# Token-wise input projection in six groups of 432 columns, with the 16 step columns inside the sixth

## The chip, the cores and the metric

The kernel runs on one core of a Trainium2 chip. The time is device microseconds of one launch, median of several runs; less is better. The engines are named as in the profile: PE is TensorE (PEld its weight loads), DVE is VectorE, ACT is ScalarE, POOL is GpSimd, and SP only issues DMA transfers and waits.

## The reference, cut to what matters

One layer of a diffusion backbone over 128 context and 1024 latent tokens. Everything is float32.

```python
h = rmsnorm(x, ln1_w) * (1 + sc1) + sh1                 # 1152 tokens x 1024
proj = h @ w_in                                         # 1024 x 3600
z, xbc, dt_raw, rq, rk, rv, rg = split(proj, [512, 1536, 1552, 2064, 2576, 3088])
xbc = silu(depthwise_conv_centred(xbc, conv_w, conv_b)) # 5 taps over tokens
dt_f = softplus(dt_raw[..., :8] + dt_bias_f)            # the 16 step columns
...                                                     # scans, w_out, PEER
```

The change touches the product `h @ w_in` alone, and there the columns outside `xbc`: z, the 16 step columns `dt_raw`, and the four retention parts, 2576 columns in all.

## The kernel before, in words

`project_in` is one block of the program (all engines meet at its start and at its end). It holds the transposed activations `hT`, eight slices of 128 features by 1152 tokens (T = 9 x 128, NT = 9). Every float32 operand is split in two, a rounded `_hi` and a remainder `_lo` (called `_rest` in the profile), and every product is three matmuls (hi x hi, hi x lo, lo x hi) for each of the KD = 8 slices: 24 matmuls to a result tile. ACT makes the `_hi` of a weight tile (`split_x`, `split_t`), DVE its remainder (`rest_x`, `rest_t`), and only then can PE use it.

The work comes in three parts, which PE does in this order.

1. *Channel blocks.* The 1024 `xbc` columns in NB = 8 blocks of 128. PE fills three PSUM banks of 384 tokens (72 matmuls), banks 0 to 2 for even blocks and 3 to 5 for odd ones. ACT copies them out (`copy_in`), DVE makes the convolution (`conv`, five operations), ACT the silu (`silu`), SP stores the block to `xbc_d`.
2. *Step columns.* The 16 columns `dt_raw` by themselves: for each of nine token tiles 24 matmuls of 16 moving columns, L423 (216 in all), into bank 6; weights `wd`, result `dts`.
3. *Token-wise groups.* The other 2560 columns in five groups of 512 (`group`, L436): for each of nine token tiles 24 matmuls of 512 columns into one of NQ = 3 banks; ACT copies the tile into one of three buffers `st`, SP stores it to `tok_d`. Tile 3 of a group can start once tile 0 is copied, and ACT can copy into a buffer once the store of three tiles before has landed (`st_stored`).

Each engine keeps the order of its own code. SP's order matters here: it stores all eight convolved blocks, waiting for each silu, then issues the first two loads of the modulation weights (`load_mod`, tile `wmr`), and then for each tile of the groups a further modulation load and the tile's store:

```python
for grp in range(5):
    for t in range(NT):
        if 2 <= grp * NT + t < 4 * KD:
            load_mod(grp * NT + t)          # waits until DVE is done with load n-2
        sp.wait_ge(tile_copied, grp * NT + t + 1)
        sp.dma_start(g.tok_d[...], st[t % NQ][:])
```

DVE works the 32 modulation rows off (L568) between the `rest_t` of the weight groups: after rows 7, 15 and 23 it waits for `split_t` of group 2, 3 and 4. POOL loads the weights, group j+2 when PE has finished group j. ACT does `split_t(j + 2)` after it has copied the last tile of group j.

Of the kernel before, what the change touches and what calls it, by code (L numbers as in the profile page):

```python
# [39 lines left out]
TC = PROJ - XBC  # L40
# [242 lines left out]
def twin(nc, ctx, name, shape):  # L283

    off = nc.sbuf_base
    assert off % 32 == 0
    whole = ctx.enter_context(nc.sbuf_tensor(name, shape, F32))
    return whole, nc.alloc_sbuf_tensor_at(name + "_rest", shape, F32R, offset=off)


def project_in(nc, g):
# [7 lines left out]
    NQ = 3  # L299
    with ExitStack() as ctx:  # L300
# [10 lines left out]
        wt, wt_lo = zip(*(twin(nc, ctx, f"wt{i}", [P, KD, 512]) for i in range(2)))  # L311
        wt_hi = [sb(f"wt_hi{i}", [P, KD, 512], F32R) for i in range(2)]
        (wd, wd_lo), wd_hi, dts = twin(nc, ctx, "wdt", [P, KD, 16]), sb("wdt_hi", [P, KD, 16], F32R), sb("dts", [P, NT, 16])
        st = [sb(f"st{i}", [P, 512]) for i in range(NQ)]
        padded, chain_sem, chain_sem_v = sem("padded"), sem("chain"), sem("chainv")
        small, wd_loaded, wx_loaded, wt_loaded = g.pi_small, g.pi_wd, g.pi_wx, g.pi_wt
# [3 lines left out]
        dt_done, dt_copied, dt_stored = sem("dt"), sem("dtcopied"), sem("dtstored")  # L320
        tile_done, tile_copied, group_done = sem("tile"), sem("tilecopied"), sem("group")
        st_stored = [sem(f"st{i}") for i in range(NQ)]
        wv = g.w_in.rearrange("(k p) n -> p k n", p=P)
# [6 lines left out]
        wx_hi_ready, wx_lo_ready, wd_hi_ready, wd_lo_ready, wt_hi_ready, wt_lo_ready = (  # L330
            sem(n) for n in ("wxhi", "wxlo", "wdhi", "wdlo", "wthi", "wtlo"))
# [4 lines left out]
        def groups(eng, body):  # L336

            body(0, 0)
            with eng.Fori(0, 2) as i:
                body(i * 2 + 1, 1)  # L340
                body(i * 2 + 2, 0)

        @block.gpsimd
        def _(pool):
            for s in range(2):
                for a, b in ((0, PAD), (PAD + P, 3 * PAD + P), (WID - PAD, WID)):
                    pool.memset(pre[s][:, a:b], 0.0).then_inc(padded, 1)
            pool.dma_start(cw[:], g.conv_w_cols).then_inc(small, 16)
            pool.dma_start(cb[:], g.conv_b_cols).then_inc(small, 16)
            for s in range(2):  # L350
                pool.dma_start(wx[s][:], wv[:, :, 512 + s * P:512 + (s + 1) * P]).then_inc(wx_loaded[s], 16)
            pool.dma_start(wd[:], wv[:, :, 512 + XBC:REST0]).then_inc(wd_loaded, 16)
            pool.dma_start(wt[0][:], wv[:, :, 0:512]).then_inc(wt_loaded[0], 16)
            pool.dma_start(wt[1][:], wv[:, :, REST0:REST0 + 512]).then_inc(wt_loaded[1], 16)
            with pool.Fori(0, NB // 2 - 1) as i:
                for s in range(2):
                    pool.wait_ge(block_done, i * 2 + s + 1)
                    pool.dma_start(wx[s][:], wv[:, :, bass.ds(i * (2 * P) + (512 + (2 + s) * P), P)]).then_inc(wx_loaded[s], 16)
            for j in range(3):
                pool.wait_ge(group_done, j + 1)  # L360
                c = REST0 + (j + 1) * 512
                pool.dma_start(wt[j % 2][:], wv[:, :, c:c + 512]).then_inc(wt_loaded[j % 2], 16)

        @block.sync
        def _(sp):
            for seq in range(2):
                sp.dma_start(cb2[:, seq], bcast_rows(g.c_rows[seq])).then_inc(mod_small, 16)
            sp.dma_start(bcol[:], g.b_mod_cols).then_inc(mod_small, 16)
            sp.dma_start(lnc[:], g.ln_cols[:, 1]).then_inc(mod_small, 16)
            for s in range(2):  # L370
                sp.sem_inc(cv_stored[s], 16)
            for s in range(NQ):
                sp.sem_inc(st_stored[s], 16)
            with sp.Fori(0, NB // 2) as i:
                for s in range(2):
                    sp.wait_ge(silu_done, i * 2 + s + 1)
                    sp.dma_start(g.xbc_d[bass.ds(i * (2 * P) + s * P, P), :], cv[s][:]).then_inc(cv_stored[s], 16)
            sp.wait_ge(dt_copied, 1)
            sp.dma_start(g.tok_d[:, 5 * 512:].rearrange("(t p) c -> p t c", p=P), dts[:]).then_inc(dt_stored, 16)

            def load_mod(n):
                if n >= 2:
                    sp.wait_ge(mod_done, 2 * (n - 1))
                sp.dma_start(wm[n % 2][:], g.w_modT[n]).then_inc(wm_loaded[n % 2], 16)
            load_mod(0)
            load_mod(1)
            for grp in range(5):
                for t in range(NT):
                    if 2 <= grp * NT + t < 4 * KD:
                        load_mod(grp * NT + t)  # L390
                    sp.wait_ge(tile_copied, grp * NT + t + 1)
                    sp.dma_start(g.tok_d[t * P:(t + 1) * P, bass.ds(grp * 512, 512)], st[t % NQ][:]).then_inc(st_stored[t % NQ], 16)
# [7 lines left out]
            sp.wait_ge(dt_stored, 16)  # L400
            for s in range(NQ):
                sp.wait_ge(st_stored[s], 16 * (5 * NT // NQ + 1))

        @block.tensor
        def _(pe):
# [12 lines left out]
            pe.wait_ge(wd_lo_ready, 1)  # L418
            for t in range(NT):
                rows = slice(t * P, (t + 1) * P)  # L420
                for k in range(KD):
                    for m, (h, w) in enumerate(((h_hi, wd_hi), (h_hi, wd_lo), (g.hT_lo, wd_hi))):
                        mm = pe.matmul(g.ps[6][:, 16 * t:16 * t + 16], h[:, k, rows], w[:, k, :],  # L423
                                       start=(k == 0 and m == 0), stop=(k == KD - 1 and m == 2))
            mm.then_inc(dt_done, 1)
            pe.wait_ge(banks_free, NB + 2)

            def group(grp, s):
                pe.wait_ge(wt_lo_ready, grp + 1)
# [19 lines left out]
        def _(act):  # L449
# [42 lines left out]
            act.wait_ge(wd_loaded, 16)  # L492
            act.activation(wd_hi[:], wd[:], ACT.Copy).then_inc(wd_hi_ready, 1)
# [10 lines left out]
            def group(grp, s):  # L504
                for t in range(NT):
                    act.wait_ge(tile_done, grp * NT + t + 1)
                    act.wait_ge(st_stored[t % NQ], grp * (16 * NT // NQ) + (t // NQ) * 16 + 16)
                    act.activation(st[t % NQ][:], g.ps[t % NQ][:], ACT.Copy).then_inc(tile_copied, 1)
            for grp in range(5):
                group(grp, grp % 2)  # L510
                if grp < 3:
                    split_t(grp + 2)

        @block.vector
        def _(dve):
# [38 lines left out]
            dve.wait_ge(wd_hi_ready, 1)  # L554
            dve.tensor_tensor(wd_lo[:], wd[:], f(wd_hi[:]), ALU.subtract).then_inc(wd_lo_ready, 1)
# [6 lines left out]
            for j in range(2, 6):  # L562
# [7 lines left out]
                if j < 5:  # L570
                    rest_t(j)
# [14 lines left out]
def decay_terms(nc, g):  # L586
# [4 lines left out]
    with ExitStack() as ctx:  # L591
# [17 lines left out]
        def _(sp):  # L609
            for dst, src in ((x[:, 0:NT, :], g.tok_d[:, 5 * 512:].rearrange("(t p) c -> p t c", p=P)),  # L610
# [1373 lines left out]
def program(nc, g, ctx):  # L1984
# [3 lines left out]
    g.pi_small, g.pi_wd, g.pi_wx, g.pi_wt = sem("pi_small"), sem("pi_wd"), [sem(f"pi_wx{i}") for i in range(2)], [sem(f"pi_wt{i}") for i in range(2)]  # L1988
# [130 lines left out]
```

## Time and profile before

| | us |
|---|---|
| median of 3 runs | 3805.85 (3803.96 to 3814.33) |
| the profiled execution: its own time | 3806.96 |
| the profiled execution: span of the core | 3805.2 |
| `project_in` within the span | about 78 to 491 |
| PE busy | 3415.7 (90%) |
| DVE busy | 2887.7 (76%) |
| ACT busy | 1418.4 (37%) |

Times in the profile are microseconds from the start of the span. The granted clock (PEclk) is the share of 2.4 GHz that PE was given: 1.00 is 2.4 GHz and 0.50 is 1.2 GHz. An idle entry such as "8.53 <-PE ps L423" says that the engine sat idle for 8.53 us until that work released it.

### The profile page before, as it was taken

The numbers are of one execution on the slowest core, as the hardware profiler recorded it, in microseconds if no ns is written. First come the engines' busy times: TensorE is split into PE (matmuls) and PEld (weight loads), VectorE is DVE, ScalarE is ACT, GpSimd is POOL, SyncE is SP. The second block draws the span as 40 slices with busy tenths as digits, with TensorE's granted clock in tenths as the row PEclk, the third lists the DMA queues.
The fourth block names the chain that finished last, engine by engine and source line by source line (L and its number), as shares of the span: only waits on it lengthen the run. The fifth ranks groups of instructions, "written<-read, shape, count | busy, mean of one in ns | idle before, by whom it ended". The sixth has DMA issues, their size and how long they took to land. (4 is left out here: it accounts for less than half of the span.)

```text
span 3805.2 us, 52216 instructions
## 1 busy us (share of the span) xinstructions
PE 3415.7 (90%) x17854; PEld 2993.1 (79%) x17854; DVE 2887.7 (76%) x4884; ACT 1418.4 (37%) x2552; POOL 1770.8 (47%) x1003
## 2 busy tenths in 40 slices
PE   5999969697999999999889899997997998989998
PEld 2998859444999999899888888996776776767776
DVE  4544247595578899998999999657886888878886
ACT  2321135243222222224777777523332333333332
POOL 0000012110211778786888888765554654555510
PEclk8979989798999999999999999998998999999999
DMA  5225334542112778776989888879999999989976
GB/s 197 74 84 180 114 105 144 167 143 80 34 34 66 233 247 257 242 262 230 341 331 348 329 342 334 329 271 356 361 384 358 354 357 353 363 327 375 371 270 210
DMA packets 416593, 947.30 MB, mean 249 GB/s; under 512 B 38035, under 2 KB 230211, under 8 KB 413267
## 3 DMA queue, kind: packets, MB, share of 16 engines
q1 hardware_dynamic: 293252, 457.63, 35.9%
q0 software_dynamic: 114480, 417.47, 29.9%
q10 hardware_dynamic: 8736, 70.78, 4.8%
q8 instruction: 48, 0.79, 0.1%
q14 instruction: 77, 0.62, 0.1%
HBM read 807.65 MB, written 138.11 MB: 249 GB/s over the span
## 5 line engine op out<-in xcount | busy, mean ns | idle before, releaser
L1872 POOL DMA_INDIRECT hT<-peer_v,hT x336 | 595.6, 1773 | 487.3 <-DVE hrow L1884 408.1
L1725 PE MATMUL ps<-h_hi,u_hi 128*128 128x384 f32 x2048 | 699.0, 341 | 31.0 <-POOL u_lo L1611 23.2
L1725 PE MATMUL ps<-h_lo,u_hi 128*128 128x384 f32 x2048 | 689.0, 336 | 0.0
L1725 PE MATMUL ps<-h_hi,u_lo 128*128 128x384 f32 x2048 | 689.0, 336 | 0.0
L1962 PE MATMUL ps<-v_hi,a_hi 128*128 128x512 f32 x1512 | 487.2, 404 | 125.8 <-DVE ga_rest L1896 114.9
L1962 PE MATMUL ps<-vw_rest,a_hi 128*128 128x512 f32 x1512 | 476.4, 397 | 0.0
L1962 PE MATMUL ps<-v_hi,ga_rest 128*128 128x512 f32 x1512 | 474.6, 396 | 0.0
L1962 PEld LDWEIGHTS ps<-v_hi,a_hi 128*128 128x128 f32 x1512 | 283.3, 193 | 219.6 <-DVE vw_rest L1894 147.0
L1842 ACT ACTIVATE v_hi<-vw 128x1024 fp32r<-128x1024 f32 x256 | 270.6, 1057 | 410.9 <-DMA vw<-peer_v 399.1
L1607 POOL DMA_INDIRECT hT<-u_rows,hT x224 | 376.0, 1679 | 95.8 <-issue 51.2
L1884 DVE SCALAR_TENSOR_TENSOR hrow<-hT,dots,hrow 128x1024 f32<-128x1024 f32 x336 | 420.4, 1279 | 0.0
L1611 POOL TENSOR_TENSOR u_lo<-uw,u_hi 128x1024 fp32r<-128x1024 f32 x126 | 341.7, 2712 | 160.8 <-ACT u_hi L1518 159.6
L1725 PEld LDWEIGHTS ps<-h_hi,u_hi 128*128 128x128 f32 x2048 | 388.2, 190 | 34.8 <-issue 32.0
L1725 PEld LDWEIGHTS ps<-h_lo,u_hi 128*128 128x128 f32 x2048 | 388.4, 190 | 0.0
L1725 PEld LDWEIGHTS ps<-h_hi,u_lo 128*128 128x128 f32 x2048 | 387.7, 189 | 0.0
L1962 PEld LDWEIGHTS ps<-vw_rest,a_hi 128*128 128x128 f32 x1512 | 290.9, 192 | 63.3
L1632 DVE CUSTOM_DVE_ANT_0 hT<-hT,hrow 128x1024 f32<-128x1024 f32 x224 | 314.0, 1446 | 33.2 <-DMA hT<-u_rows,hT 32.1
L1962 PEld LDWEIGHTS ps<-v_hi,ga_rest 128*128 128x128 f32 x1512 | 289.6, 192 | 62.9
L1523 ACT ACTIVATE so<-ps 128x384 f32<-128x384 f32 x256 | 123.8, 484 | 544.0 <-PE ps L1725 417.8
L1892 DVE TENSOR_TENSOR ga<-ga,gt 128x384 f32<-128x384 f32 x256 | 142.0, 555 | 241.0 <-DMA ga<-s_d 239.1
L1894 DVE TENSOR_TENSOR vw_rest<-vw,v_hi 128x1024 fp32r<-128x1024 f32 x256 | 312.3, 1220 | 9.7 <-ACT v_hi L1842 8.6
L1691 DVE TENSOR_TENSOR hT<-iota,sel 128x1024 f32<-128x1024 f32 x192 | 302.7, 1616 | 6.4 <-ACT sel L1546 6.4
(336 smaller groups left out, 6040.2 us busy)
## 6 DMA issues: line engine op xcount, KB each, us to landing
vw<-peer_v SPq DMA_DIRECT2D x256, 512.0 KB, 8.5
uw<-u_T SPq DMA_DIRECT2D x128, 512.0 KB, 4.3
s_d<-so SPq DMA_DIRECT2D x256, 192.0 KB, 5.0
gates_d<-big ACTq DMA_DIRECT2D x24, 2048.0 KB, 10.0
gt<-gates_d SPq DMA_DIRECT2D x64, 768.0 KB, 8.8
ga<-s_d SPq DMA_DIRECT2D x256, 192.0 KB, 8.8
wmr<-w_modT SPq DMA_DIRECT2D x32, 512.0 KB, 4.0
tok_d<-st SPq DMA_DIRECT2D x45, 256.0 KB, 2.2
```

The source lines that it names most:

```text
L1523: act.activation(so[b][:], g.ps[4 + 2 * s + b][:, 0:HALF], ACT.Gelu_apprx_tanh).then_inc(act_done, 1)
L1607: pool.indirect_dma_start(rows[slot], None, table, bass.IndirectOffsetOnAxis(ap=g.pick[q][:, i:i + 1], axis=0)).then_inc(row_loaded[slot], 16)
L1611: pool.tensor_tensor(u_lo[e % 2][:], uw[e % 2][:], f(u_hi[e % 2][:]), ALU.subtract).then_inc(u_lo_ready, 1)
L1632: z = dve.tensor_tensor_reduce(rows[slot], rows[slot], g.hrow[:, n // NSEL], 1.0, 0.0, ALU.mult, ALU.add, g.dots[:, n // NSEL, n % NSEL:n ...
L1691: z = dve.tensor_tensor(hot, numbers, sel3[:, i, r * G:(r + 1) * G].unsqueeze(2).broadcast_to([P, G, P]), ALU.is_equal)
L1725: mm = pe.matmul(g.ps[4 + 2 * s + b][:, 0:HALF], u[s][:, k, :], h[:, k, b * HALF:(b + 1) * HALF], start=(k == 0 and i == 0), stop=(k == KD ...
L1842: act.activation(v_hi[s][:], vw[s][:], ACT.Copy).then_inc(v_hi_ready, 1)
L1872: pool.indirect_dma_start(rows[n % NU], None, g.v_rows, bass.IndirectOffsetOnAxis(ap=g.pick[m % GT][:, m // GT:m // GT + 1], axis=0)).then ...
L1884: dve.scalar_tensor_tensor(g.hrow[:, q], rows[n % NU], g.dots[:, q, i:i + 1], g.hrow[:, q], ALU.mult, ALU.add).then_inc(added, 1)
L1892: dve.tensor_tensor(by, by, gt[n // RING % 2][:, 0:(c1 - c0) // CT, s * CT:(s + 1) * CT], ALU.mult).then_inc(a_ready, 1)
L1894: dve.tensor_tensor(v_lo[s][:], vw[s][:], f(v_hi[s][:]), ALU.subtract).then_inc(v_lo_ready, 1)
L1962: mm = pe.matmul(g.ps[bank(p, t) + q][:], aa[s][:, rows_], v[s][:, q * 512:(q + 1) * 512], start=(begin and i == 0), stop=(end and i == 2) ...
```

## The change

The step columns lose their own pass. The 2576 columns outside `xbc`, with the step columns last and 16 columns of zeros behind them, make six groups of 432 (`TW`). The zeros and the new order of columns are laid out ahead of the launch, in two inputs `w_xbc` and `w_tok` in place of `w_in`. So there are 54 tiles of 24 matmuls of 432 columns in place of 45 tiles of 512 and the 216 matmuls of 16. Ahead of group 0 PE waits until channel block 6 (of 0 to 7) is copied out of banks 0 to 2 (`banks_free` NB + 1), and no longer until block 7 is. ACT copies the first three tiles of group 0 ahead of the last silu.

```diff
@@ -37,7 +37,8 @@
-TC = PROJ - XBC
+TW = 432
+TC = 6 * TW
...
         def groups(eng, body):
 
             body(0, 0)
-            with eng.Fori(0, 2) as i:
+            body(1, 1)
+            with eng.Fori(1, NG // 2) as i:
+                body(i * 2, 0)
                 body(i * 2 + 1, 1)
-                body(i * 2 + 2, 0)
...
             for s in range(2):
-                pool.dma_start(wx[s][:], wv[:, :, 512 + s * P:512 + (s + 1) * P]).then_inc(wx_loaded[s], 16)
-            pool.dma_start(wd[:], wv[:, :, 512 + XBC:REST0]).then_inc(wd_loaded, 16)
-            pool.dma_start(wt[0][:], wv[:, :, 0:512]).then_inc(wt_loaded[0], 16)
-            pool.dma_start(wt[1][:], wv[:, :, REST0:REST0 + 512]).then_inc(wt_loaded[1], 16)
+                pool.dma_start(wx[s][:], wv[:, :, s * P:(s + 1) * P]).then_inc(wx_loaded[s], 16)
+            for j in range(2):
+                pool.dma_start(wt[j][:], tv[:, :, j * TW:(j + 1) * TW]).then_inc(wt_loaded[j], 16)
...
-            for j in range(3):
-                pool.wait_ge(group_done, j + 1)
-                c = REST0 + (j + 1) * 512
-                pool.dma_start(wt[j % 2][:], wv[:, :, c:c + 512]).then_inc(wt_loaded[j % 2], 16)
+            for j in range(2, NG):
+                pool.wait_ge(group_done, j - 1)
+                pool.dma_start(wt[j % 2][:], tv[:, :, j * TW:(j + 1) * TW]).then_inc(wt_loaded[j % 2], 16)
...
-            sp.wait_ge(dt_copied, 1)
-            sp.dma_start(g.tok_d[:, 5 * 512:].rearrange("(t p) c -> p t c", p=P), dts[:]).then_inc(dt_stored, 16)
...
-            pe.wait_ge(wd_lo_ready, 1)
-            for t in range(NT):
-                rows = slice(t * P, (t + 1) * P)
-                for k in range(KD):
-                    for m, (h, w) in enumerate(((h_hi, wd_hi), (h_hi, wd_lo), (g.hT_lo, wd_hi))):
-                        mm = pe.matmul(g.ps[6][:, 16 * t:16 * t + 16], h[:, k, rows], w[:, k, :],
-                                       start=(k == 0 and m == 0), stop=(k == KD - 1 and m == 2))
-            mm.then_inc(dt_done, 1)
-            pe.wait_ge(banks_free, NB + 2)
+            pe.wait_ge(banks_free, NB + 1)
...
             copy_in(NB - 2, 0, NB // 2 - 1)
-            act.wait_ge(wd_loaded, 16)
-            act.activation(wd_hi[:], wd[:], ACT.Copy).then_inc(wd_hi_ready, 1)
             split_t(0)
             silu(NB - 2, 0, NB // 2 - 1)
             copy_in(NB - 1, 1, NB // 2 - 1)
             split_t(1)
+
+            def group(grp, tiles):
+                for t in tiles:
+                    act.wait_ge(tile_done, grp * NT + t + 1)
+                    act.wait_ge(st_stored[t % NQ], grp * (16 * NT // NQ) + (t // NQ) * 16 + 16)
+                    act.activation(st[t % NQ][:], g.ps[t % NQ][:, 0:TW], ACT.Copy).then_inc(tile_copied, 1)
+            group(0, range(NQ))
             silu(NB - 1, 1, NB // 2 - 1)
             act.wait_ge(mod_small, 64)
             act.activation(cb2[:], cb2[:], ACT.Silu).then_inc(mod_silu, 1)
-            act.wait_ge(dt_done, 1)
-            act.activation(dts[:], g.ps[6][:, 0:16 * NT].rearrange("p (t c) -> p t c", t=NT), ACT.Copy).then_inc(dt_copied, 1)
...
-            for grp in range(5):
-                group(grp, grp % 2)
-                if grp < 3:
+            for grp in range(NG):
+                group(grp, range(NQ if grp == 0 else 0, NT))
+                if grp + 2 < NG:
                     split_t(grp + 2)
...
-            dve.wait_ge(wd_hi_ready, 1)
-            dve.tensor_tensor(wd_lo[:], wd[:], f(wd_hi[:]), ALU.subtract).then_inc(wd_lo_ready, 1)
...
-            for dst, src in ((x[:, 0:NT, :], g.tok_d[:, 5 * 512:].rearrange("(t p) c -> p t c", p=P)),
+            for dst, src in ((x[:, 0:NT, :], g.tok_d[:, 5 * 512:5 * 512 + 16].rearrange("(t p) c -> p t c", p=P)),
...
-        "w_in": A["w_in"][0],
+        "w_xbc": f(A["w_in"][0][:, 512:512 + XBC]),
+        "w_tok": f(np.concatenate([A["w_in"][0][:, 0:512], A["w_in"][0][:, REST0:], A["w_in"][0][:, 512 + XBC:REST0],
+                                   np.zeros((D, TC - (PROJ - XBC)), np.float32)], 1)),
```

PE, at the end of the channel blocks (ps5 is the last bank of block 7, ps6 was the bank of the step columns). Before:

```order
L415 MATMUL ps5<-hT_rest_49,wx_hi1 128x384
L415 MATMUL ps5<-pi_h_hi,wx1_rest_498 128x384
L406 REGISTER_ALU
L406 COMPARE_AND_BRANCH
L423 MATMUL ps6<-wdt_hi,pi_h_hi 128x16 [waits pi_wdlo]
L423 MATMUL ps6<-wdt_rest_501,pi_h_hi 128x16
```

And PE at the same place now:

```order
L410 MATMUL ps5<-hT_rest_49,wx_hi1 128x384
L410 MATMUL ps5<-pi_h_hi,wx1_rest_498 128x384
L401 REGISTER_ALU
L401 COMPARE_AND_BRANCH
L423 MATMUL ps0<-wt_hi0,pi_h_hi 128x432 [waits pi_wtlo,pi_banksfree]
L423 MATMUL ps0<-wt0_rest_499,pi_h_hi 128x432
```

The first tile of group 0 now stands right behind the last channel block, where the 216 matmuls of the step columns stood.

ACT, from the split of group 0's weights on (wt0 and wt1 are the weights of groups 0 and 1, cv0 and cv1 the convolved blocks 6 and 7; between them block 7 is copied out). Before:

```order
L493 ACTIVATE wdt_hi<-wdt 128x128 [waits pi_pre,pi_wd]
L458 ACTIVATE wt_hi0<-wt0 128x4096 [waits pi_wt0]
L481 ACTIVATE cv0<-acc0,cb 128x128 [waits pi_cvst0,pi_conv]
...
L458 ACTIVATE wt_hi1<-wt1 128x4096 [waits pi_pre,pi_wt1]
L481 ACTIVATE cv1<-acc1,cb 128x128 [waits pi_cvst1,pi_conv]
L482 ACTIVATE cv1<-acc1,cb 128x1024
L500 ACTIVATE cboth<-cboth 128x2048 [waits pi_chain,pi_msmall]
L502 ACTIVATE dts<-ps6 128x144 [waits pi_dt]
```

And ACT at the same place now:

```order
L445 ACTIVATE wt_hi0<-wt0 128x3456 [waits pi_pre,pi_wt0]
L468 ACTIVATE cv0<-acc0,cb 128x128 [waits pi_cvst0,pi_conv]
...
L445 ACTIVATE wt_hi1<-wt1 128x3456 [waits pi_pre,pi_wt1]
L488 ACTIVATE st0<-ps0 128x432 [waits pi_st0,pi_tile]
L488 ACTIVATE st1<-ps1 128x432 [waits pi_st1,pi_tile]
L488 ACTIVATE st2<-ps2 128x432 [waits pi_st2,pi_tile]
L468 ACTIVATE cv1<-acc1,cb 128x128 [waits pi_cvst1,pi_conv]
L469 ACTIVATE cv1<-acc1,cb 128x1024
```

Three tile copies moved ahead of the last silu; the split of `wdt` and the copy of `dts` are gone.

SP, behind the loop that stores the convolved blocks. Now it reads (before, one more row, the store of `dts`, stood ahead of the first `wmr` load):

```order
L375 DMA xbc_d<-cv1 128x1152
L372 REGISTER_ALU
L372 COMPARE_AND_BRANCH
L380 DMA wmr0<-w_modT 128x1024
L380 DMA wmr1<-w_modT 128x1024
L388 DMA tok_d<-st0 128x432 [waits pi_tilecopied]
L388 DMA tok_d<-st1 128x432 [waits pi_tilecopied]
```

SP's order did not move with ACT's: the stores of the first tiles still stand behind the store of the last convolved block.

## Rows read from the trace of the kernel before

**Rows 1.** The page: its first line.

```profile
span 3805.2 us, 52216 instructions
```

**Rows 2.** Instructions by line: PE, times in ns min/median/max, then first and last start.

```profile
L423 PE MATMUL ps<-wdt_hi,pi_h_hi x72: 170/361/362, 194.3 to 236.1; 128*128 128x16 f32 x72
L436 PE MATMUL ps<-wt_hi,pi_h_hi x360: 388/388/774, 236.8 to 489.2; 128*128 128x512 f32 x180
```

**Rows 3.** Busy time by stretch: length, busy (count) per engine, PEclk, DMA share, GB/s.

```profile
88.30:92.30 4.00, 3.97 (x12) 3.97 (x13) 2.60 (x1) 4.00 (x3) 0.00 (x0) 0.50 1.02 419
92.30:198.10 105.80, 102.49 (x600) 101.53 (x599) 53.53 (x41) 36.79 (x55) 5.34 (x6) 1.00 0.24 83
198.10:236.90 38.80, 38.80 (x184) 38.80 (x185) 19.53 (x12) 9.72 (x10) 0.00 (x0) 0.50 0.08 31
236.90:242.50 5.60, 5.60 (x15) 4.34 (x15) 0.57 (x1) 0.29 (x1) 0.00 (x0) 0.50 0.71 199
```

**Rows 4.** Timeline of ACT: start, length, operation, count, [idle before it, who ended it].

```profile
192.07 0.31 ACT L493 ACTIVATE wdt_hi<-wdt 128x128 fp32r<-128x128 f32 x1
192.29 3.61 ACT L458 ACTIVATE wt_hi<-wt 128x4096 fp32r<-128x4096 f32 x1
...
210.14 3.62 ACT L458 ACTIVATE wt_hi<-wt 128x4096 fp32r<-128x4096 f32 x1
...
225.18 1.13 ACT L482 ACTIVATE cv<-acc,cb 128x1024 f32<-128x1024 f32 x1
```

**Rows 5.** Timeline of ACT in the groups: the copies of tiles.

```profile
245.24 0.60 ACT L508 ACTIVATE st<-ps 128x512 f32<-128x512 f32 x1 [8.01 <-PE ps L436]
250.73 0.60 ACT L508 ACTIVATE st<-ps 128x512 f32<-128x512 f32 x1 [4.89 <-PE ps L436]
...
490.12 0.60 ACT L508 ACTIVATE st<-ps 128x512 f32<-128x512 f32 x1 [4.89 <-PE ps L436]
```

**Rows 6.** Timeline of POOL: loads issued when channel blocks 1 and 2 are done.

```profile
116.08 0.88 POOL L358 DMA_DIRECT2D wx<-w_in  x1 [11.55 <-PE ps L415]
128.58 0.88 POOL L358 DMA_DIRECT2D wx<-w_in  x1 [11.61 <-PE ps L415]
```

**Rows 7.** Timeline of DVE: the remainders of groups 0 and 1, the last convolution.

```profile
195.93 4.43 DVE L525 TENSOR_TENSOR wt_rest<-wt,wt_hi 128x4096 fp32r<-128x4096 f32 x1 [3.22 <-ACT wt_hi L458]
...
213.79 4.43 DVE L525 TENSOR_TENSOR wt_rest<-wt,wt_hi 128x4096 fp32r<-128x4096 f32 x1 [6.87 <-ACT wt_hi L458]
...
218.98 5.80 DVE L544 SCALAR_TENSOR_TENSOR acc<-pre,cw,acc 128x1156 f32<-128x1156 f32 x4
```

**Rows 8.** Timeline of SP: last block's store, first modulation loads; then load 26.

```profile
226.53 0.33 SPq L377 DMA_DIRECT2D xbc_d<-cv  x1
...
237.69 1.07 SPq L384 DMA_DIRECT2D wmr<-w_modT  x2
...
408.36 0.33 SPq L384 DMA_DIRECT2D wmr<-w_modT  x1
```

**Rows 9.** Page, DMA issues: transfer, size, median us to landing.

```profile
tok_d<-st SPq DMA_DIRECT2D x45, 256.0 KB, 2.2
```

**Rows 10.** Timeline of ACT at the end of group 2 (tile 26) and behind it.

```profile
389.54 0.60 ACT L508 ACTIVATE st<-ps 128x512 f32<-128x512 f32 x1 [4.90 <-PE ps L436]
397.96 3.63 ACT L458 ACTIVATE wt_hi<-wt 128x4096 fp32r<-128x4096 f32 x1 [7.83 <-DMA wt<-w_in]
...
413.31 0.60 ACT L508 ACTIVATE st<-ps 128x512 f32<-128x512 f32 x1 [10.75 <-DMA tok_d<-st]
416.51 0.60 ACT L508 ACTIVATE st<-ps 128x512 f32<-128x512 f32 x1 [2.60 <-DMA tok_d<-st]
```

**Rows 11.** Tile wt, issue to landing of the five weight loads.

```profile
DMA to landing us min/median/max: 8.0/10.3/14.4
```

**Rows 12.** Tile wx, 70 to 200 us: waits that its load ended (us, times).

```profile
  DMA wx<-w_in: 8.6, 2
```

**Rows 13.** Waits in 190 to 495 us: total, times, longest.

```profile
ACT st L508 <- DMA tok_d<-st: 22.9, 4, 10.8
```

More of the change, by code:

```diff
@@ L299, in project_in @@
     NQ = 3
+    NG = TC // TW
     with ExitStack() as ctx:
@@ L310, in project_in @@
         cw, cb = sb("cw", [P, NB, TAPS]), sb("cb", [P, NB])
[L311 to L314, printed above, removed]
+        wt, wt_lo = zip(*(twin(nc, ctx, f"wt{i}", [P, KD, TW]) for i in range(2)))
+        wt_hi = [sb(f"wt_hi{i}", [P, KD, TW], F32R) for i in range(2)]
+        st = [sb(f"st{i}", [P, TW]) for i in range(NQ)]
         padded, chain_sem, chain_sem_v = sem("padded"), sem("chain"), sem("chainv")
-        small, wd_loaded, wx_loaded, wt_loaded = g.pi_small, g.pi_wd, g.pi_wx, g.pi_wt
+        small, wx_loaded, wt_loaded = g.pi_small, g.pi_wx, g.pi_wt
         block_done, banks_free, pre_ready, pre_free = sem("block"), sem("banksfree"), sem("pre"), sem("prefree")
@@ L319, in project_in @@
         cv_stored = [sem("cvst0"), sem("cvst1")]
-        dt_done, dt_copied, dt_stored = sem("dt"), sem("dtcopied"), sem("dtstored")
         tile_done, tile_copied, group_done = sem("tile"), sem("tilecopied"), sem("group")
         st_stored = [sem(f"st{i}") for i in range(NQ)]
-        wv = g.w_in.rearrange("(k p) n -> p k n", p=P)
+        wv, tv = (w.rearrange("(k p) n -> p k n", p=P) for w in (g.w_xbc, g.w_tok))
         wm, cb2 = [sb(f"wmr{i}", [P, D]) for i in range(2)], sb("cboth", [P, 2, D])
@@ L329, in project_in @@
         h_hi_ready, h_lo_ready = sem("hhi"), sem("hlo")
-        wx_hi_ready, wx_lo_ready, wd_hi_ready, wd_lo_ready, wt_hi_ready, wt_lo_ready = (
-            sem(n) for n in ("wxhi", "wxlo", "wdhi", "wdlo", "wthi", "wtlo"))
+        wx_hi_ready, wx_lo_ready, wt_hi_ready, wt_lo_ready = (sem(n) for n in ("wxhi", "wxlo", "wthi", "wtlo"))
         f = lambda ap: ap.bitcast(F32)
@@ L391, in _ @@
                     sp.wait_ge(tile_copied, grp * NT + t + 1)
-                    sp.dma_start(g.tok_d[t * P:(t + 1) * P, bass.ds(grp * 512, 512)], st[t % NQ][:]).then_inc(st_stored[t % NQ], 16)
+                    sp.dma_start(g.tok_d[t * P:(t + 1) * P, grp * TW:(grp + 1) * TW], st[t % NQ][:]).then_inc(st_stored[t % NQ], 16)
             sp.wait_ge(mod_rows, 1)
@@ L431, in group @@
                     rows = slice(t * P, (t + 1) * P)
-                    if not (isinstance(grp, int) and t < NQ):
+                    if not (isinstance(grp, int) and grp * NT + t < NQ):
                         pe.wait_ge(tile_copied, grp * NT + (t - NQ + 1))
@@ L435, in group @@
                         for m, (h, w) in enumerate(((h_hi, wt_hi), (h_hi, wt_lo), (g.hT_lo, wt_hi))):
-                            mm = pe.matmul(g.ps[t % NQ][:], h[:, k, rows], w[s][:, k, :],
+                            mm = pe.matmul(g.ps[t % NQ][:, 0:TW], h[:, k, rows], w[s][:, k, :],
                                            start=(k == 0 and m == 0), stop=(k == KD - 1 and m == 2))
@@ L500, in _ @@
             act.activation(cb2[:], cb2[:], ACT.Silu).then_inc(mod_silu, 1)
-            act.wait_ge(dt_done, 1)
-            act.activation(dts[:], g.ps[6][:, 0:16 * NT].rearrange("p (t c) -> p t c", t=NT), ACT.Copy).then_inc(dt_copied, 1)
[L504 to L509, printed above, removed]
-                group(grp, grp % 2)
-                if grp < 3:
+            for grp in range(NG):
+                group(grp, range(NQ if grp == 0 else 0, NT))
+                if grp + 2 < NG:
                     split_t(grp + 2)
@@ L1987, in program @@
     sem = lambda n: new_sem(nc, ctx, n, lasting)
-    g.pi_small, g.pi_wd, g.pi_wx, g.pi_wt = sem("pi_small"), sem("pi_wd"), [sem(f"pi_wx{i}") for i in range(2)], [sem(f"pi_wt{i}") for i in range(2)]
+    g.pi_small, g.pi_wx, g.pi_wt = sem("pi_small"), [sem(f"pi_wx{i}") for i in range(2)], [sem(f"pi_wt{i}") for i in range(2)]
     g.hg_rows, g.ou_rows = [sem(f"hg_row{i}") for i in range(16)], [sem(f"ou_row{i}") for i in range(NU)]
```

8 lines of the change are left out of this document (3 added, 5 removed).

## Prediction

> **What bounds the kernel now.** I read the page's first line, then the lines of PE, then the stretches of `project_in`, and last the timelines of ACT, DVE and SP around its weak places. The profiled execution took 3806.96 us for a span of 3805.2 [rows 1], 1.1 us over the median of 3805.85. `project_in` ends with all engines meeting, so what PE gains in it should be gained at the end, unless a later stage gives it back.
>
> The step columns hold PE from 194.3 to 236.8 [rows 2]: 42.5 us for 216 matmuls of 16 columns. The reader should see in [rows 3] what they do to the clock: 1.00 up to 198.1, 0.50 until 236.9, and still 0.50 for 5.6 us after the wide matmuls have begun. The groups follow until the last tile is copied at 490.12 [rows 5]. Tiles are 5.49 us apart (245.24, 250.73), 228.9 ns for each of 24 matmuls. From the first copy to the last, 244.88 us hold 44 tiles (241.7) and four joints between groups, 3.2 together. So PE bounds the groups and almost nothing stalls it.
>
> **The change, part by part.**
>
> *Removed: the step columns.* Their 42.5 us go, with the slow start of group 0 behind them (its first copy comes 8.4 us after 236.8, not 5.5: 2.9 us). The split of `wdt` (0.31 [rows 4]), its load, and the copy and store of `dts` lay beside other work; I count them as 0 except the 0.22 us that ACT was later for it (192.29 for 192.07).
>
> *Wider in number, narrower each: the tiles.* No row has 432 columns. Those of 384 are in the channel blocks: 12.50 us from block 1 to block 2 [rows 6] for 72 matmuls, 173.6 ns each. A line from there to 228.9 at 512 gives 194.3 ns at 432, a tile of 4.66 us. The bounds are in proportion to columns from either end, 4.63 and 4.69. So 54 tiles take 251.6 us where 45 took 247.2: +4.4 us (2.8 to 6.1).
>
> The page "TensorE: Matmul & The Clock Gate" of the Trainium skill (Back-to-back issue gap) has columns over 2.4 GHz and 2.5 ns for every matmul. By it 54 tiles would take 236.5 us and 45 tiles 233.1, a difference of 3.4 in place of 4.4. Its 215.8 ns for 512 columns is below the 228.9 of this trace, so the trace agrees that a fixed part is small, not with the size.
>
> *The new start of group 0.* PE is done with block 7 at 194.3 and then waits for the remainder of group 0's weights. ACT starts their split at 192.07, in 3.61 x 432/512 = 3.05 us; DVE's remainder [rows 7] takes 4.43 x 432/512 = 3.74; so PE starts at 192.07 + 3.05 + 3.74 + 0.1 = 198.95. Block 6 was copied out before 192.07, so the bank wait is free. PE idles 4.65 us. Tiles 0 to 5 end at 198.95 + 6 x 4.66 = 226.9.
>
> *ACT's first tiles.* DVE was free of group 0's remainder at 200.36 and will be at 198.9: what follows from it comes 1.46 us earlier. The split of group 1's weights starts at 208.7 (was 210.14 [rows 4]) and ends at 211.75. Tile 2 ends at 212.9, so all three copies are made by 213.5, tiles 3 to 5 need no wait, and the last silu is not late for it: DVE's second remainder ends at 215.5, and the last convolution, which ended 6.56 us behind that (224.78 against 218.22 [rows 7]), at 222.1. The silu ended 1.53 us behind it (226.31 [rows 4]), now at 223.7.
>
> *The new wait, on SP's queue.* ACT can copy tile 3 only when the store of tile 0 has left buffer 0, and SP issues that store behind the last convolved block and two modulation loads. By its spacing in [rows 8] (block 0.2 after the silu, two loads in 1.07): block 223.9, loads 224.3 and 224.9, tile 0 at 225.4. When it lands no row shows. Not before 225.4 + 2.2 [rows 9] = 227.6, if it passes the loads. From above: load 26 issued at 408.36 [rows 8] and the store behind it ended ACT's wait at 413.31, the next pair at 416.51 [rows 10]: 4.95 us for 768 KB and 3.2 for each further 768. Block, loads and store are 1816 KB from 223.9, so 4.95 + 1048/240 = 9.3, landing at 233.2. I take 231.0, nearer the upper end, since it is queued behind the loads. ACT's copy is done at 231.65; PE needed it at 226.9 for tile 6. **Stall 4.75 us** (1.4 to 6.9). Behind this copy on ACT are those of tiles 4 and 5; their stores follow at once or some 5 us later, and PE needs them 4.66 and 9.3 us later, in time.
>
> *The clock after the two gaps.* Gaps in the channel blocks left 1.00 [rows 3]; longer idle time ahead of 88.3 and the step columns left 0.50 for 4.0 and 5.6 us of work, which costs half, 2.0 to 2.8. A fall after the first gap is hidden, since tile 6 waits for the store anyway; one after the second is not. I take half its price, 1.2.
>
> The same page (Why this matters for your kernels) tells authors to leave no idle gaps between bursts of matmuls, or the clock falls back. Its rule speaks against this change, which makes two gaps where there was none. By it both gaps cost, and the sum is 1.2 us worse than mine, 3778; which gap is long enough no run here shows yet.
>
> *Later groups.* The tightest place is tile 32, the sixth of group 3. It needs tile 29's copy, that the store of tile 26, that load 26, that DVE's row 24, that the remainder of group 4's weights, whose load starts as group 2 ends. Before: group end 389.54, split 397.96, load 26 at 408.36, copy at 413.31, done 24.4 us after the end; PE came at 0.8 + 5 x 5.49 = 28.3, a joint and five tiles. Now split and remainder are 1.25 shorter and the load about 1.2, so 22.0, and PE comes after 0.8 + 5 x 4.66 = 24.1. Slack 2.1 us, for a load 8.0 long [rows 11]. At 10.9 it would be overrun by 0.3 us, at 14.4 by 3.3.
>
> *At nothing.* The channel blocks' weights now come from rows 4096 bytes apart in place of 14400, and group weights in pieces of 1728 bytes in place of 2048. Only two `wx` loads ended a wait (8.6 us [rows 12]); the others hide behind DVE and ACT. A load 1 us longer or shorter costs or gives 2 us. The modulation rows end long before PE does.
>
> **Sum.** Tile 6 starts at 231.7; 48 tiles take 223.7 and five joints 4.0 (the four had 3.2): 459.4, and 460.6 with the clock's 1.2. Against 490.1 that is 29.5 us less: 3806.96 - 29.5 = 3777.5. I put 3777.
>
> **The rivals.**
>
> 1. *SP's queue is not late* (13%). The store passes the loads and lands near 227.6; tile 6 starts at 228.3, and the clock stays high. Then PE ends at 456.0, 34.1 less: **3772.9**. For it: a tile store alone takes 2.2 us. Against it: with a load ahead, ACT waited up to 10.8 us for one [rows 13].
>
> 2. *The waits spread* (20%). Store at 233.2 (+2.2), the whole fall of the clock (+1.6), and loads of weights as long as the long ones in [rows 11], with 3.3 at tile 32 and about 1 elsewhere: +8.1, **3785.6**. For it: ACT already waited 22.9 us in four such places [rows 13]; its cover shrinks with the tile. Against it: PE still has 2 us there, and the traffic per group is smaller.
>
> 3. *A matmul of 432 columns costs what one of 512 does* (3%), the case on the other side. Each tile then takes 5.49: tile 6 starts at 231.9 and 48 tiles take 263.5, PE ends at 499.4 and with the clock's 1.2 at 500.6: +10.5 us, **3817**. It decides from (490.1 - 460.6)/1152 = 26 ns more per matmul, 220 ns. Against it: 384 columns take 173.6, on the line through 512 and nearly nothing.
>
> 4. *Loads from the new rows are much slower* (2%). Only two are on the path now; the others must first use up their cover. To eat 29.5 us all eight must land at least 29.5/8 = 3.7 us later, and more by what the six now have in hand. About **3800** to 3810. Against it: the same bytes in the same number of pieces.
>
> My forecast has 62%, with a range of its own from 3772 to 3783.
>
> **How the numbers follow.** Rivals 1 and 2 lie on either side and are both faster; 3 and 4 are left out of the range. The stages behind 491 us run the same instructions, but three runs of before spread from 3804 to 3814, so a few us are added: 3768 to 3790. What can be told from no change is 0.3%, 11.4 us, so faster means below 3794: my forecast and rivals 1 and 2, 95%, less 1 for a later stage that gives it back. Same 3%, slower 3% (rival 3).
>
> **What the changed profile would show.** The first wide matmul near 199 after a gap of 4.65; 4.66 us between copies; tile 3's copy near 231 with a wait that ends on a transfer of `tok_d`; a second gap of PE of 1 to 7 us ahead of tile 6; the last copy near 460; no stall of PE in group 3. Wrong if copies are over 4.75 apart, if the second gap is absent or above 7, or if the span behind the last copy is not about 3315 us, as it was (3805.2 - 490.1).

## The result and the profile after

| | median us | lowest to highest | runs | profiled execution | span |
|---|---|---|---|---|---|
| before | 3814.06 | 3803.96 to 3818.05 | 10 | 3806.96 | 3805.2 |
| changed | 3788.77 | 3778.29 to 3798.79 | 10 | 3781.83 | 3780.2 |

The ratio is 0.9939 (95%: 0.9922 to 0.9956): faster, by more than the 0.3% that can be told. The medians differ by 25.3 us and the two profiled executions by 25.1; the forecast was 28.9. The median lies outside the range that the forecast gave itself, 3772 to 3783, and inside the wider 3768 to 3790. Two things differ from the forecast, and they are kept apart below: the saving, a few us smaller, and the level of both kernels. The seven runs added for the kernel before lifted its median by 8.2 us, from 3805.85 to 3814.06.

First the stage of the change. The windows of the changed kernel from the end of the last channel block on (length, busy time and count for PE, PEld, DVE, ACT, POOL, then PEclk, DMA share, GB/s); they answer to [rows 3]:

```profile
194.30:198.97 4.67, 0.05 (x1) 0.03 (x1) 3.90 (x2) 0.73 (x1) 0.00 (x0) 0.91 0.00 0
198.97:204.70 5.73, 5.73 (x16) 5.28 (x17) 5.59 (x5) 0.00 (x0) 0.00 (x0) 0.50 0.00 0
204.70:229.95 25.25, 25.25 (x130) 24.04 (x128) 11.24 (x8) 10.59 (x13) 0.00 (x0) 0.99 0.25 87
229.95:232.04 2.09, 0.17 (x2) 0.00 (x1) 2.09 (x5) 0.56 (x2) 0.00 (x0) 1.00 0.61 231
232.04:235.60 3.56, 3.56 (x10) 3.26 (x11) 2.21 (x4) 0.51 (x1) 0.00 (x0) 0.54 0.73 172
```

The 38.8 us at half clock and the slow start behind them are gone. In their place stand two gaps of PE, and behind each a stretch at 0.50 and 0.54, the level of 1.2 GHz for all or nearly all of it. The first wide matmul and the second gap, from the timeline of PE in the same trace:

```profile
198.97 0.70 PE L423 MATMUL ps<-wt_hi,pi_h_hi 128*128 128x432 f32 x1 [4.62 <-DVE wt_rest L509]
...
232.04 0.53 PE L423 MATMUL ps<-wt_hi,pi_h_hi 128*128 128x432 f32 x1 [1.93 <-ACT st L488]
```

The wait behind that gap, from the timeline of ACT:

```profile
211.62 0.93 ACT L488 ACTIVATE st<-ps 128x432 f32<-128x432 f32 x2
216.11 0.53 ACT L488 ACTIVATE st<-ps 128x432 f32<-128x432 f32 x1 [3.56 <-PE ps L423]
...
222.47 1.14 ACT L469 ACTIVATE cv<-acc,cb 128x1024 f32<-128x1024 f32 x1
...
231.46 1.09 ACT L488 ACTIVATE st<-ps 128x432 f32<-128x432 f32 x2 [5.75 <-DMA tok_d<-st]
```

and the timeline of SP, whose queue the store of tile 0 stood in; it answers to [rows 8]:

```profile
223.82 0.33 SPq L375 DMA_DIRECT2D xbc_d<-cv  x1
224.37 1.25 SPq L380 DMA_DIRECT2D wmr<-w_modT  x2
225.66 0.93 SPq L388 DMA_DIRECT2D tok_d<-st  x2
```

ACT had copied tile 0 before 213, but SP issued its store at 225.66, behind the last convolved block and two loads, and ACT stood still until 231.46 (forecast 231.0). The copy was early, but its store was not. The rest of the stage is steady, as [rows 5] was; ACT's copies:

```profile
277.15 0.53 ACT L488 ACTIVATE st<-ps 128x432 f32<-128x432 f32 x1 [3.43 <-PE ps L423]
281.83 0.53 ACT L488 ACTIVATE st<-ps 128x432 f32<-128x432 f32 x1 [4.15 <-PE ps L423]
...
356.71 0.53 ACT L488 ACTIVATE st<-ps 128x432 f32<-128x432 f32 x1 [9.89 <-DMA tok_d<-st]
...
462.76 0.53 ACT L488 ACTIVATE st<-ps 128x432 f32<-128x432 f32 x1 [4.15 <-PE ps L423]
```

Tiles are 4.68 us apart, and the last copy is at 462.76 where it was at 490.12, 27.4 us earlier in the span. Counted from the start of the projection, which came 0.4 us earlier (78.0 for 78.4), the stage is 26.9 us shorter. Behind the last copy the span goes on for 3317.4 us, where it went on for 3315.1: 2.3 us less saved at the end.

### The profile page after: what moved, and what is told of

The parts are those of the page before. It is cut to its first block and busy times, and to the rows that moved or that the text cites. A ratio compares the mean times of both kernels' runs of the same rounds, so it can differ in the third digit from the quotient of the medians.

```text
span 3780.2 us, 52243 instructions
## 1 busy us (share of the span) xinstructions
PE 3380.7 (89%) x17854; PEld 2991.9 (79%) x17854; DVE 2888.3 (76%) x4884; ACT 1418.9 (38%) x2560; POOL 1746.4 (46%) x1003
## 5 line engine op out<-in xcount | busy, mean ns | idle before, releaser
L1853 POOL DMA_INDIRECT hT<-peer_v,hT x336 | 575.6, 1713 | 509.3 <-DVE hrow L1865 434.6
L1943 PEld LDWEIGHTS ps<-v_hi,a_hi 128*128 128x128 f32 x1512 | 284.4, 193 | 220.9 <-DVE vw_rest L1875 131.1
```

What stands on the lines that cost most here:

```text
L1853: pool.indirect_dma_start(rows[n % NU], None, g.v_rows, bass.IndirectOffsetOnAxis(ap=g.pick[m % GT][:, m // GT:m // GT + 1], axis=0)).then ...
L1943: mm = pe.matmul(g.ps[bank(p, t) + q][:], aa[s][:, rows_], v[s][:, q * 512:(q + 1) * 512], start=(begin and i == 0), stop=(end and i == 2) ...
```

## The experiments

Each profile is cut at one place, the last tile copy. "Stage" is the time from the start of the input projection to that copy, and "behind" the rest of the span. "Outputs" is the last stage of the program, part of "behind", and "DVE waits" what DVE stands still in it for the loads of `ga`. Medians compare only within a row: groups of kernels ran on different chips, each beside the kernel before on the same chip. Ahead of the stage lie 78.0 to 82.5 us in the twelve profiles.

| kernel | median, runs | before it | ratio (95%) | stage | behind | outputs | DVE waits |
|---|---|---|---|---|---|---|---|
| before | 3814.06, 10 | | | 411.7 | 3315.1 | 1227.8 | 219.2 |
| before_again | 3815.6, 1 | | | 412.2 | 3321.4 | 1233.3 | 225.0 |
| before_third | 3818.2, 1 | | | 412.0 | 3325.2 | 1236.8 | 227.4 |
| changed | 3788.77, 10 | 3814.06 | 0.9939 (0.9922 to 0.9956) | 384.8 | 3317.4 | 1230.5 | 221.7 |
| after_again | 3802.48, 12 | 3822.11 | 0.9939 (0.9914 to 0.9965) | 386.1 | 3308.5 | 1217.2 | 207.8 |
| early | 3794.37, 6 | 3822.11 | 0.9916 (0.9885 to 0.9947) | 372.9 | 3329.3 | 1239.8 | 231.2 |
| sp_first | 3791.12, 6 | 3822.11 | 0.9912 (0.9879 to 0.9944) | 381.9 | 3331.5 | 1247.1 | 238.3 |
| act_undo | 3803.38, 10 | 3822.11 | 0.9951 (0.9925 to 0.9977) | 392.4 | 3327.0 | 1238.4 | 229.8 |
| one_step | 3796.9, 10 | 3823.0 | 0.9946 (0.9920 to 0.9972) | 385.7 | 3327.8 | 1239.5 | 231.1 |
| one_step_order | 3780.93, 4 | 3823.0 | 0.9895 (0.9855 to 0.9935) | 376.0 | 3318.8 | 1230.1 | 220.9 |
| fill | 3783.6, 1 | | | 386.8 | 3314.2 | 1225.9 | 217.5 |
| both | 3781.54, 6 | 3820.02 | 0.9901 (0.9865 to 0.9937) | 374.0 | 3327.0 | 1237.5 | 229.1 |

The intervals of the ratios all overlap: the medians show that each of these kernels is faster than the one before, and not which of them is fastest. What follows is read from the stage, one profile to a kernel; the stage repeats within 1.3 us in two profiles of the changed kernel and within 0.5 in three of the kernel before.

### early: the splits ahead of the channel blocks

The edit to the changed kernel, on ACT and the same on DVE:

```diff
             act.wait_ge(small, 32)
+            split_t(0)
+            split_t(1)
...
-            split_t(0)
             silu(NB - 2, 0, NB // 2 - 1)
             copy_in(NB - 1, 1, NB // 2 - 1)
-            split_t(1)
...
             dve.wait_ge(small, 32)
+            rest_t(0)
+            rest_t(1)
...
-            rest_t(0)
             conv(NB - 2, 0)
-            rest_t(1)
             conv(NB - 1, 1)
```

> The changed kernel with the splits of the weights of groups 0 and 1 (ACT and DVE) moved ahead of the first channel block, where both engines idle. Theory A, the ledger of the prediction as measured (gap of 4.6 us, then the store of tile 0 late on SP, then two falls of the clock): PE goes straight from block 7 at 194 into group 0, every later step of ACT, DVE and SP comes 7 to 10 us earlier (last silu near 210, tile 0 stored near 217), no wait at tile 6; 54 tiles of 4.68 and joints of 4.2: last copy at 451, 12 us before the changed kernel's 462.8. Rival B, that only the removal of the step columns matters and the gaps are made good by slack later on: last copy at 461 to 463. Time: A 0.3% under the changed kernel, 0.9% under the kernel before; B as the changed kernel.

Its windows over the same work, with the same columns:

```profile
194.00:200.00 6.00, 6.00 (x35) 5.96 (x35) 3.57 (x3) 1.95 (x5) 0.00 (x0) 1.00 0.24 98
...
222.00:262.00 40.00, 39.70 (x204) 37.87 (x203) 24.96 (x38) 8.20 (x11) 0.88 (x1) 1.00 0.65 198
```

PE is busy all the way and the clock stays at 1.00. The stage takes 372.9 us, 11.9 less than the changed kernel's. The store wait on ACT is still there (its copy of tile 3 is at 222.67, after 5.79 us idle for `tok_d`), but ACT's and DVE's work ahead of it is shorter, so it ends before PE needs the bank. The two gaps and what the clock lost behind them were 12 us that PE could have worked: 4.62 and 1.93 us of idle time, 2.9 and 1.6 us lost at the lower clock, 11.1 of the 11.9.

### after_again: the changed kernel once more

No edit.

> The changed kernel once more, beside the kernel before on the same chip, for the level that the prediction missed. Theory A: inside the groups nothing varies but the clock; last copy at 462 to 464 again, and the stages behind differ from run to run by several us with the clock that PE is granted in them, so the ratio is again 0.992 to 0.995, while both absolute medians may lie anywhere within 10 us of the first ones. Rival B: the later stages systematically give back some 2 to 4 us of the gain; then the span behind the last copy is again at least 3317 against 3315 of before.

The stage repeats within 1.3 us (386.1 and 384.8), the ratio to four digits. Behind the last copy it takes 3308.5 us, less than the kernel before (3315.1): nothing there gives the saving back. On this chip the medians of both kernels are higher than in the first comparison, by 8.1 (before) and 13.7 us (changed).

### sp_first: the first stores ahead of the last block and the loads

```diff
-            with sp.Fori(0, NB // 2) as i:
+            with sp.Fori(0, NB // 2 - 1) as i:
...
+            sp.wait_ge(silu_done, NB - 1)
+            sp.dma_start(g.xbc_d[(NB - 2) * P:(NB - 1) * P, :], cv[0][:]).then_inc(cv_stored[0], 16)
+            for t in range(NQ):
+                sp.wait_ge(tile_copied, t + 1)
+                sp.dma_start(g.tok_d[t * P:(t + 1) * P, 0:TW], st[t][:]).then_inc(st_stored[t], 16)
+            sp.wait_ge(silu_done, NB)
+            sp.dma_start(g.xbc_d[(NB - 1) * P:NB * P, :], cv[1][:]).then_inc(cv_stored[1], 16)
...
+                    if grp * NT + t < NQ:
+                        continue
```

> The changed kernel with SP storing tiles 0 to 2 of group 0 ahead of the last convolved block and the modulation loads. Theory A (tile 6 waits for the store of tile 0 behind the block and two loads): tile 3 is copied as soon as ACT is through with the last silu and cboth, near 225.8, and PE goes from tile 5 (230.2 after the first fall of the clock) into tile 6 without a gap and without the second fall: the last copy 1.9 + 1.7 = 3.6 us earlier, 459.1. Rival B (tile 6 waits for ACT, not for the store): ACT's copy of tile 3 stays near 231.5 and the last copy at 462.8. Rival C: the modulation rows now start later and push DVE's remainders, so that a later group stalls: last copy at 461 or more though the first wait is gone.

The timeline of ACT in this kernel, with tiles 3 and 4, then tile 6:

```profile
226.07 0.93 ACT L497 ACTIVATE st<-ps 128x432 f32<-128x432 f32 x2
...
238.89 0.54 ACT L497 ACTIVATE st<-ps 128x432 f32<-128x432 f32 x1 [7.89 <-DMA tok_d<-st]
```

Tile 3 is copied at 226.07 behind no transfer, the second gap and the second fall of the clock are gone (from 226 to 262 us PE works 35.42 of 36.00 us at a granted clock of 1.00), and the stage is 2.9 us shorter than the changed kernel's (4.2 against its repeat). That is the price of SP's order. The wait has moved three tiles on, to a store behind the modulation loads, where PE has more in hand.

### act_undo: the last silu first again

```diff
-            group(0, range(NQ))
             silu(NB - 1, 1, NB // 2 - 1)
...
             act.activation(cb2[:], cb2[:], ACT.Silu).then_inc(mod_silu, 1)
+            group(0, range(NQ))
```

> The changed kernel with ACT's first three tile copies put back behind the last silu and the silu of cboth, the order of before. Theory A: tile 3 cannot start before ACT has done cboth at 225.7, and copies tile 0 at 226.3; PE idles from 216.1 for 10 us, the clock falls again (1.7 to 2.8 us), tiles 3 to 5 end near 242 to 243, tile 3's store wait is over by then; last copy 8 to 11 us later, 471 to 474. The silu comes no earlier, since it waits for DVE. Rival B (ACT is free enough; DVE's silu order does not matter): within 2 us of 462.8.

PE now waits at tile 3, for the copy of tile 0:

```profile
229.02 0.73 PE L423 MATMUL ps<-wt_hi,pi_h_hi 128*128 128x432 f32 x1 [10.08 <-ACT st L488]
```

The stage is 392.4 us, 6.3 to 7.6 more than the changed kernel's two runs. The mechanism is as expected, its price a little below the 8 us that were expected at least. The order on ACT is thus worth about 7 of the 27 us by which the changed stage is shorter.

### one_step and one_step_order: the old kernel with a ninth of the step pass

Both start from the kernel before. one_step:

```diff
-            for t in range(NT):
+            for t in range(1):
                 rows = slice(t * P, (t + 1) * P)
...
-            act.activation(dts[:], g.ps[6][:, 0:16 * NT].rearrange("p (t c) -> p t c", t=NT), ACT.Copy).then_inc(dt_copied, 1)
+            act.activation(dts[:], g.ps[6][:, 0:16].unsqueeze(1).broadcast_to([P, NT, 16]), ACT.Copy).then_inc(dt_copied, 1)
```

one_step_order has this as well, and the waits and the order of ACT of the changed kernel:

```diff
-            pe.wait_ge(banks_free, NB + 2)
+            pe.wait_ge(banks_free, NB + 1)
...
             split_t(1)
+            for t in range(NQ):
+                act.wait_ge(tile_done, t + 1)
+                act.wait_ge(st_stored[t], 16)
+                act.activation(st[t][:], g.ps[t][:], ACT.Copy).then_inc(tile_copied, 1)
             silu(NB - 1, 1, NB // 2 - 1)
...
-                for t in range(NT):
+                for t in range(NQ if grp == 0 else 0, NT):
```

> The kernel before with the pass of the step columns cut to the first token tile, 24 matmuls of 216; its result is used for all nine tiles, so eight ninths of that product are left out. Five groups of 512, the order of before. Theory A: the price of the pass itself. PE now waits until block 7 is copied out (210.1) for group 0, ACT copies tile 0 only after cboth and dts (228.8), so tile 3 starts near 229.4 and the last copy is near 463.5, 26.6 us before 490.1 and about the same as the changed kernel. Rival B: what counts is the PE time taken away, 38 us and the 2.9 of the slow start: last copy at 449 to 452.

> The same with the changed kernel's two changes of order: PE waits for block 6 only, and ACT copies three tiles ahead of the last silu. Theory A: group 0 starts at 200.4, one fall of the clock (2.9), no wait at tile 6 (tile 5 ends at 236, tile 0's store lands near 234), last copy near 454, so the order is worth 9 to 10 us and 54 narrow tiles with their wait at tile 6 cost 9 us against 45 wide ones. Rival B: the order is worth nothing beside the removed pass: last copy as in the run without it.

Without eight ninths of the step pass the old kernel's stage falls from 411.7 to 385.7 us, which is all that the change reached. PE then stands still for 13.06 us ahead of group 0, until ACT has copied block 7 out. With the two changes of order the stage falls by 9.7 more, to 376.0; this kernel changes the bank that PE waits for as well as ACT's order, so the 9.7 are the price of both.

From there to the changed kernel, which has tiles of 432 columns in place of 512 and no step pass at all, it is 8.8 to 10.1 us up again. The 54 narrow tiles account for 5.5 of it (below). The first gap is not the rest: group 0 starts 121.7 us into the stage here (200.83 less 79.1) and 121.0 in the changed kernel (198.97 less 78.0), and the clock falls to 0.50 behind both gaps (3.44 and 4.62 us). They differ at tile 6, whose row in one_step_order is

```profile
237.16 0.50 PE L436 MATMUL ps<-wt_hi,pi_h_hi 128*128 128x512 f32 x1 [1.02 <-ACT st L512]
```

A wait was not expected there. But it is 1.02 us in place of 1.93, and the granted clock stays at 1.00 in the 3.60 us behind it, where the changed kernel lost 1.6 us: 2.5 us together. The copy that frees the bank is later here (157.4 us into the stage, against 153.5), but six tiles of 5.49 us cover more of the wait than six of 4.68. Narrower tiles thus cost twice: by their sum, and by what they no longer cover. The last 0.8 us is not taken apart.

### fill: matmuls in the first gap

The changed kernel with 26 more matmuls, whose result is thrown away:

```diff
+            for j in range(26):
+                pe.matmul(g.ps[6][:, 0:TG], wx_hi[1][:, j % KD, :], h_hi[:, j % KD, 0:TG], start=(j == 0), stop=(j == 25))
             pe.wait_ge(banks_free, NB + 1)
```

> The changed kernel with 26 matmuls of 384 columns into an unused bank in the gap between block 7 and group 0 (their result is thrown away). Theory A: the clock stays at 1.00 through the gap, tiles 0 to 5 end near 227 in place of 230, but tile 6 still starts at 232 behind the store of tile 0: a gap of near 5 us, a fall behind it, last copy at 462.5 to 464, no gain. Rival B: the fall of the clock behind the first gap is what the 1.1 us over the ledger and more came from: last copy 2.5 to 3 us earlier, 460.

The windows of the first gap and of the first six tiles, then PE's second gap from the timeline:

```profile
190.00:199.00 9.00, 9.00 (x54) 9.00 (x53) 2.29 (x3) 5.86 (x7) 0.00 (x0) 1.00 0.16 66
199.00:234.00 35.00, 31.48 (x163) 29.76 (x161) 20.87 (x13) 10.59 (x13) 0.00 (x0) 1.00 0.21 71
```

```profile
235.31 0.73 PE L425 MATMUL ps<-wt_hi,pi_h_hi 128*128 128x432 f32 x1 [4.71 <-ACT st L490]
```

The first fall of the clock is gone and nothing is gained by it (stage 386.8): PE comes to tile 6 earlier and waits there for the same copy, 4.71 us in place of 1.93. So the first fall was hidden behind the store's wait, as the prediction had put it.

### both: early and sp_first together

> The changed kernel with both edits that took a wait away: the splits of the first two groups ahead of the channel blocks (run early) and SP's three early stores (run sp_first). Theory A: they are not additive, since in the run early PE never waited at tile 6. From the start of the projection to the last copy 373 us, as in early (372.9), against 384.8 to 386.8 of the changed kernel; the ratio to before 0.989 to 0.993. Rival B (the two gains add): 369 to 370 us.

The stage is 374.0 us, as in early alone (372.9), so the two don't add up: once the splits are early, the store's wait holds nobody. The median is 38.5 us below the kernel before beside it (0.9901), and of the kernels that compute the whole reference this is the lowest; from early, at 0.9916 (0.9885 to 0.9947) on another chip, it can't be told apart.

### before_again and before_third: the kernel before, two more profiles

No edit.

> The kernel before once more, for one more profile. Theory A: the part up to the last copy repeats within 1 us (411.7 from the start of the projection), and the stages behind it do not: the last stage, which took 1228 us before and 1217 to 1247 in eight profiles of other kernels, and the part from the start of the token mixing to the scores (233.0 before, 235 to 237 in all others) differ again, so that the span behind the last copy is anywhere from 3305 to 3335. Rival B (the change slows the token mixing by 3 us, since its rows of tok_d are 10368 bytes apart in place of 10304): that part takes 233 again.

> The same kernel and the same expectations as before_again: theory A 235 to 237 us from the start of the token mixing to the scores at least once in the two profiles, rival B 233 in both.

The stage repeats within 0.5 us. What is behind it does not: 3315.1, 3321.4 and 3325.2 us for the same instructions. From the waits of DVE in the last stage, first of after_again, then of sp_first (line waited for: us in total, times, longest):

```profile
DVE ga L1873 <- DMA ga<-s_d: 207.8, 77, 13.4
```

```profile
DVE ga L1882 <- DMA ga<-s_d: 238.3, 76, 13.7
```

Nearly as many waits, and the longest about the same, but 30.5 us more in all, and the outputs stage is 29.9 us longer. Down the last two columns of the table the order is the same for all twelve profiles, whichever kernel it is.

## Why the prediction was right or wrong

**The mechanism held.** The step pass went with its slow start; PE had its first gap of 4.62 us (forecast 4.65) and started group 0 at 198.97 (198.95); the new wait stood on SP's queue and ended at 231.46 (231.0); the three early copies kept the last silu on time (223.6, forecast 223.7). The stall of 4.75 us that the prediction counts from 226.9 is there too, in two parts: 2.9 us of it went into the slow first tiles, and 1.93 were left as the gap. Rival 1, that SP's queue is not late, is ruled out by rows: ACT stood 5.75 us for the store. Rival 3 is too: a matmul of 432 columns takes 4.68/24 = 195 ns, not 229. Against rival 4, the loads of `wx` from the new rows land in 4.5 us at the median, as before, and two of them ended waits of 8.8 us in all, for 8.6. Rival 2, the waits spread, has the price next to the median (3785.6), but that is luck: the fall of the clock came whole, as it says, but the store was 0.3 us late and not 2.2, and the loads cost PE 0.35 us and not 4.3. ACT did wait more for stores, 61.3 us in 15 places for 22.9 in four; at one of them, tile 6, PE waited too.

**"The clock after the two gaps".** The step said that a fall after the first gap is hidden and one after the second is not. fill shows the first half, and sp_first, with no second gap, the second. The term that was mis-sized is the second fall: taken as half of 2.0 to 2.8, since it might not come; it came and cost 0.46 x 3.56 = 1.6 us. The Trainium skill, "TensorE: Matmul & The Clock Gate" (Why this matters for your kernels), warns of idle gaps between bursts of matmuls. This trace agrees for the first gap, of 4.62 us. The second, of 1.93 us, is shorter than the gaps that its warning is for, and there the measurement decides: 0.54 for 3.56 us. What closing both brings, early shows.

**"Wider in number, narrower each".** 4.66 us for a tile was 0.02 short; over the 48 tiles from tile 6 on that is 1.0 us. 54 tiles cost 252.7 against 247.2, +5.5 for +4.4.

**"Later groups".** The load of a group's weights was counted about 1.2 us shorter for its fewer bytes. It isn't. The statistics of tile wt in the changed kernel give, over the loads of the groups' weights from 180 us on,

```profile
DMA to landing us min/median/max: 7.9/9.4/10.9
```

where the three of before in the same stretch took 8.0 to 10.9, median 9.0; with the early loads the median is 10.3 in both, as in [rows 11]. The first of them took 10.9 us and left a stall at tile 12, whose first matmul starts 0.54 us behind the one before it (262.25 and 262.79) and not 0.195: 0.35 us. At the tightest place, tile 32, the copy it needs (356.71) was done 23.2 us after the end of group 2, not 22.0, and PE came at 23.9 (357.93 less 334.07): of the slack of 2.1 us a third was left, and the conclusion, no stall in group 3, held.

Together 0.3 (store, tile 6 at 232.04 for 231.7), 0.4 (clock), 1.0 (tiles) and 0.35 (tile 12) give 2.1 us, and the last copy was 2.2 us later than forecast (462.76 for 460.6). These are the terms of the saving that were off: 27.4 us at the last copy in place of 29.5.

**"How the numbers follow": the step that failed.** The level was taken from one profiled execution near the median of three runs, and "a few us are added" for the stages behind, which "run the same instructions". Those stages make most of the spread: the outputs stage alone lay between 1217 and 1247 us in twelve profiles with the same work in it, while the changed stage repeats within 1.3. The median of before rose to 3814, and was 3820 to 3823 in the other comparisons. Of the 11.8 us between forecast (3777) and median (3788.77), 8.2 are this level and 3.6 the saving (25.3 for 28.9), of which the stage explains 2.1. The median is 5.8 us above the forecast's own range of 3772 to 3783. It is inside 3768 to 3790, but only just, and the changed kernel's own median in the second comparison, 3802.5, is outside. A ratio would have been right: 3777/3805.85 = 0.9924 lies in the interval measured, at its lower end. In microseconds the range had to hold the spread of ten and more runs, whose farthest runs lie 10 to 25 us from their median, not that of three. For the same reason the last sign in the prediction, a span of about 3315 us behind the last copy, could not tell right from wrong: it was 3315 to 3325 in three profiles of before.

**A later stage that gives it back** was given 1%. The 2.3 us more behind the last copy look like it, but after_again has 6.6 less than before. Over the profiles the mean behind is 3320.6 us for three of before and 3322.1 for seven of kernels with 432 columns. Open stays a possible 1 to 2 us in the token mixing right behind the stage: from its start to the scores it takes 233.0, 233.5 and 235.4 us in the profiles of before, and 235.2 to 236.7 in those of the 432-column kernels; but one_step and one_step_order, with 512, have 235.2 and 235.5.

**What stays open.** Why the loads of `ga` are slower in one execution than in the next. The granted clock of that stage goes along with it (mean 0.97 in after_again, 0.95 in sp_first), but which of the two causes the other, or whether a third thing moves both, no run here tells apart.

## What to carry to other kernels

When a block of matmuls is removed, look for what it covered: here it covered a wait for split weights and one for a late store, which cost 12 us once they lay bare, and moving the splits to where ACT and DVE have time gave those back. Follow a copy that is moved forward down to the queue of the DMA that frees its buffer; the copy was early, its store was not. And forecast a ratio or a difference, and take the spread in microseconds from many executions of the stages that you don't touch, above all those that wait for transfers. Narrower work of the same sum covers less: a wait that six tiles of 5.49 us all but hid was 1.93 us long behind six of 4.68, and the clock fell behind it.

## What was not expected of the hardware

- A gap of 1.93 us ahead of 232.04 left the granted clock at 0.54 for the next 3.56 us. The same place in after_again, 2.00 us, left 0.54 for 3.57. Gaps of 1.57 and 1.32 us in the channel blocks (ahead of 167.50 and 181.59), and one of 1.02 in one_step_order, left it at 1.00; the one of 4.62 at 0.50 for 5.73 us of work.
- Loads of a group's weights in pieces of 1728 bytes take as long as those in pieces of 2048 (median 10.3 us for both; 9.4 and 9.0 for those issued inside the groups).
- The same last stage, with transfers under way for 0.93 to 0.95 of the time, took 1217 to 1247 us from one execution to the next.
